# A three-term fp32 encoder: where the second wide tile of the next unit's scores stands

## The reference

```python
def _band_attend(q, k, v, q_pos, k_pos, rel_bias):
    s = jnp.einsum('bqhd,bkhd->bhqk', q, k, ...) * (A_HEAD_DIM ** -0.5)
    ...
    p = jax.nn.softmax(jnp.where(valid, s + bias, NEG), axis=-1)
    return jnp.einsum('bhqk,bkhd->bqhd', p, v.astype(jnp.float32))
...
y = jnp.concatenate([br, mo], axis=-1) * jax.nn.silu(gate)
x = x + y @ w_out[i]
```

## Time and profile before

| | us |
|---|---|
| median of 3 runs | 2897.47 |
| lowest and highest | 2891.87, 2906.21 |
| profiled execution | 2902.79 |
| its span | 2901.0 |
| TensorE busy | 2741.9 (95%) |
| DVE, ACT, POOL busy | 1344.6, 1326.0, 723.6 |
| granted TensorE clock, mean | 0.974 |

### The profile page before, as it was taken

The page is one execution under the profiler, slowest core; times in us unless marked ns, Lnnn a source line. Parts: engine busy times, 40 slices in busy tenths (PEclk is TensorE's granted clock), DMA queues, the critical chain, the costliest instruction groups (busy, mean ns, idle before and its releaser), DMA issues.

```text
span 2901.0 us, 46736 instructions
## 1 busy us (share of the span) xinstructions
PE 2741.9 (95%) x18936; PEld 2570.8 (89%) x18936; DVE 1344.6 (46%) x3237; ACT 1326.0 (46%) x2851; POOL 723.6 (25%) x399
## 2 busy tenths in 40 slices
PE   7999999989999999989999989999899999999897
PEld 5999999879999999979998878888799999999786
DVE  4045555564215565664515255555512055555643
ACT  4244444442325555552334356666523344444521
POOL 0232222234222222221521122222051222222313
PEclk9999999989999999989999999999899999999898
DMA  4111111114211121113311000000232111111111
GB/s 150 55 60 52 47 47 47 50 43 161 68 48 63 56 70 53 59 47 120 103 50 47 26 27 12 13 10 7 86 134 68 48 47 57 47 51 55 52 68 67
DMA packets 58629, 171.98 MB, mean 59 GB/s; under 512 B 6768, under 2 KB 15472, under 8 KB 57904
## 3 DMA queue, kind: packets, MB, share of 16 engines
q1 hardware_dynamic: 58416, 169.01, 16.9%
HBM read 135.06 MB, written 33.92 MB: 58 GB/s over the span
## 4 chain that ended last, share of the span: by engine, by line
PE 76%; ACT 9%; DVE 8%; issue 3%; POOL 3%; DMA 0%; SPq 0%; DVEq 0%; ACTq 0%
PE acc L1876 40%; PE acc L1966 11%; PE turned L1925 6%; PE scores L1909 5%; PE scores L1753 4%; PE acc L1823 4%; ACT prob L1272 3%; DVE prob L1563 2%; PE turned L1753 2%; PE scores L1898 1%; DVE pt_split L1592 1%; PE scores L1730 1%; DVE y_sb L1621 1%; ACT pt_split L1284 1%; POOL w_lo L1652 1%
## 5 line engine op out<-in xcount | busy, mean ns | idle before, releaser
L1876 PE MATMUL acc<-h_split,w_hi 128*128 128x352 f32 (+2 forms) x5220 | 986.5, 330 | 36.3 <-DVE w_rest L1484 9.3
L1876 PEld LDWEIGHTS acc<-h_split,w_hi 128*128 128x128 f32 x5220 | 852.5, 191 | 70.0 <-issue 18.1
L1652 POOL TENSOR_TENSOR w_lo<-w_raw,w_hi 128x1024 fp32r<-128x1024 f32 (+2 forms) x154 | 333.7, 2168 | 1558.6 <-ACT w_hi L1170 1558.6
L1592 DVE TENSOR_TENSOR pt_split<-turned,pt_split 128x512 fp32r<-128x512 f32 (+4 forms) x564 | 303.3, 552 | 537.3 <-ACT pt_split L1284 536.5
L1563 DVE CUSTOM_DVE_ANT_0 prob<-scores,bias 128x256 f32<-128x256 f32 (+9 forms) x576 | 338.0, 633 | 418.6 <-PE scores L1909 395.7
L1876 PE MATMUL acc<-h_split,w_lo 128*128 128x352 f32 (+2 forms) x2610 | 514.6, 325 | 0.0
L1966 PE MATMUL acc<-pt_split,v_split 128*64 128x256 f32 (+5 forms) x3486 | 480.8, 274 | 26.6 <-ACT pt_split L1284 7.9
L1272 ACT ACTIVATE prob<-prob,stat 128x256 f32<-128x256 f32 (+9 forms) x468 | 303.7, 650 | 298.6 <-DVE stat L1563 298.5
L1876 PEld LDWEIGHTS acc<-h_split,w_lo 128*128 128x128 f32 x2610 | 438.1, 190 | 0.0
L1966 PEld LDWEIGHTS acc<-pt_split,v_split 128*64 128x64 f32 (+1 forms) x3486 | 390.1, 155 | 43.9 <-ACT pt_split L1284 14.9
L1284 ACT ACTIVATE pt_split<-turned 128x512 fp32r<-128x512 f32 (+4 forms) x564 | 261.6, 482 | 248.6 <-PE turned L1925 247.5
(11 more groups left out here) (142 smaller groups left out, 2844.3 us busy)
## 6 DMA issues: line engine op xcount, KB each, us to landing
w_raw<-w SPq DMA_DIRECT2D x132, 512.0 KB, 3.7
x_scr<-y_sb SPq DMA_DIRECT2D x24, 528.0 KB, 5.6
y_sb<-x_scr SPq DMA_DIRECT2D x24, 528.0 KB, 7.9
y_sb<-x_in SPq DMA_DIRECT2D x16, 528.0 KB, 10.6
mw_raw<-w SPq DMA_DIRECT2D x16, 512.0 KB, 8.8
bias<-rel_in SPq DMA_DIRECT2D x24, 320.0 KB, 4.2
raw<-kcache SPq DMA_DIRECT2D x18, 256.0 KB, 3.9
v_cache<-vcache SPq DMA_DIRECT2D x18, 256.0 KB, 3.9
```

The costliest lines, as they stand in the source:

```text
L1592: ins = dve.tensor_tensor(pt[0:rows, chunk.p % 2, 1, c0:c0 + n], t_ps[chunk.a % 2][0:rows, c0:c0 + n], pt[0:rows, chunk.p % 2, 0, c0:c0 + ...
L1652: pool.tensor_tensor(w_lo[:, n % 2, 0:wide], w_raw[:, n % 2, 0:wide], w_hi[:, n % 2, 0:wide].bitcast(F32), ALU.subtract).then_inc(wlo_made ...
L1876: ins = pe.matmul(acc[s.bank][:, 0:s.cols], w[ws][:, 128 * k:128 * k + 128], x(xs, k), start=(k, y) == products[0], stop=(k, y) == product ...
```

## The change

One condition loses one term: the second wide tile is now placed behind the second turning in layers A and B too, wherever the present unit has more than one chunk.

```diff
@@ -460,7 +460,7 @@
         if at == 4 and following is not None:
             order.append(("bprep", following))
         narrow = two and max(t.width for t in nxt.tiles) <= 512
-        late_scores = two and not narrow and nxt.job.kind == "C" and n > 1
+        late_scores = two and not narrow and n > 1
         for c in range(n):
             if c == 0 and at == 0 and prev is not None:
                 self.times_v(prev, len(prev.chunks) - 1)
```

## The result

| | before | after |
|---|---|---|
| median of 16 runs, us | 2897.95 | 2905.11 |
| lowest and highest, us | 2891.57, 2906.21 | 2898.77, 2910.93 |
| profiled execution, us | 2902.79 | 2908.76 |
| its span, us | 2901.0 | 2907.0 |
| mean granted clock in it | 0.974 | 0.977 |

The changed kernel is slower: ratio 1.0028, 95% interval 1.0018 to 1.0038, so 5 to 11 us. The forecast was 6 us faster, and the time lies above the range (2883 to 2902). It is inside the bound of 0.5% that I called "within", but clear of the noise and of the other sign.

A forecast was written before the change was run, and what follows sets the result against it. TensorE, busy 95% of the span, was taken as the bound, leaving its idle time and low clock. Waits 2.3 us plus clock 3.7 us gave 6.0 us gained, from the 2897.5 median to 2891.5 us; range 2883 to 2902.

The forecast's parts named there:

- Zero, in all 12: Unit 0 of band jobs: no gain or loss; unit 3's first turning keeps 0.5 us of slack at full clock.
- signs of being wrong: Unit 3's turning waiting in all jobs, new side waits for the bank in jobs with a drop, or differential-layer drops.
- The clock: Band layers: about 4 of 8 clock drops go as shorter jobs slide away, 0.92 us each, 3.7 us gained; bounds 0 to 7.4.
- Third turning of full band jobs: Unit 1: its wait goes, 0.38 us in 7 jobs with a drop; net 0.23 in 3 without, after a query-read wait.
- Last band job: Unit 1, each band layer: third turning's 1.35 us wait becomes a fourth-turning wait 0.3 us dearer, 0.6 us lost in two.
- Differential jobs: Unit 1: first gains 0.3 us, middle four nothing, last loses 0.8 us at the first turning of unit 2.
- "nothing" for the swap: TensorE, all 30 places: exchanging scores and turning costs 0; some 0.2 us either way possible, widening the range by 1 us.
- (a): Rival: the clock drops stay, one in each job, and only the waits count: 2895.2 us; chance 0.2.
- (b): Rival: nearly all eight clock drops go: 2887.8 us; chance 0.15.
- (c): Rival: no effect, the third turning's wait comes back at the fourth everywhere: 2897.5 us; chance 0.09.
- (d): Rival: slower, second tile late on DVE, 0.8 us at 18 unit 1 places, 0.3 at 12 unit 0: 2915.5 us; chance 0.06.
- The rule weighed: Clock drops come from waits of the array for data; by it alone the change would leave all eight.

The follow-up runs named there:

- the three kernels: The changed kernel (0.85 us lost in unit 0), unit0_only (0.86 us a job) and sides_adjacent (0.92 us a job).
- sides_adjacent: Kernel before, with unit 0's second-tile scores in band jobs moved behind the second side and no further: 2906.59 us, ratio 1.0034.
- sides_apart: The change, but in unit 0 of the band jobs the second side stands behind the late scores: 2895.92 us, ratio 1.0000 to before.
- the first four experiments: unit1_only, unit0_only, sides_adjacent and sides_apart, run on the same chip as 21 runs of the kernel before.
- the last two: full_band_jobs and bsum_between, run on the same chip as 21 runs of the kernel before.
- unit1_only: Kernel before, with the second tile's scores late in unit 1 alone (18 places): 2894.64 us against 2896.64, ratio 0.9993.
- unit0_only: Kernel before, with the second tile's scores late in unit 0 of the 12 band jobs alone: 2905.39 us, ratio 1.0035.
- full_band_jobs: Kernel before, with the second tile late in unit 1 of the 10 full band jobs alone: 2896.28 us against 2898.10, ratio 0.999.
- bsum_between: full_band_jobs, plus the sum of squares put between second and third side in differential jobs' unit 0: 2891.66 us against before's 2898.10, ratio 0.9977.

## Why the prediction was wrong

**The step that failed: unit 0 of the band jobs.** I wrote "Zero, in all 12". I followed the moved step to its new place, asked what it would make late there (the first turning of unit 3, 0.5 us of slack) and found nothing; that part held, for no such wait is in after. I never asked what it left behind. It had been the cover of ACT's read between two sides. I even named the 24 products that it moves past, and that all sides share a bank is in the description of the code. The price could be read in advance: the row of 4.9 us in 6 times for `raw`, and its mark of 0.55 us in layer B's unit 0, where three sides stand in a row. 10 x 0.88 (the mean of the 0.85, 0.86 and 0.92 of the three kernels) = 8.8 us. That the two neighbours are the cause is shown by sides_adjacent (the loss with turning and normalising in the old order) and sides_apart (0.64 of 0.85 us gone with all the rest as in after). One of my signs of being wrong was new waits of sides for the bank; I looked for them in unit 1, and they came in unit 0.

**The clock, forecast at 3.7 us gained: no gain shown.** In the profiled executions the drops of the full band jobs fell from seven to two, and the mean granted clock rose from 0.974 to 0.977. The mechanism, that a job of another length slides away from the drops, fits this: the traces of the six experiments, one execution each, have none to four in these ten jobs. The error was to take one execution for the mean, and then to take the gain off the wrong number. I counted drops in an execution that stood 5.3 us above the median, and subtracted their price from the median. The mean granted clock over many executions, by kernel:

| runs | mean granted clock |
|---|---|
| before, beside the first four experiments (21) | 0.9778, from 0.975 to 0.981 |
| before, beside the last two (21) | 0.9766, from 0.973 to 0.980 |
| after (16) | 0.9765 |
| unit1_only (11), unit0_only (5) | 0.9768, 0.9778 |
| sides_adjacent (5), sides_apart (11) | 0.9780, 0.9776 |
| full_band_jobs (11), bsum_between (11) | 0.9773, 0.9756 |

The profiled execution of before, with 0.974, lies below all of the first 21 and near the lowest of the second. A line through the first 21 runs gives 1.5 us for each 0.001 of clock. So 3.7 us gained would be 0.0025 more clock, and after doesn't show it against either group. Nor is a loss shown: the two groups of one kernel differ by 0.0012 themselves, some 2 us. The term should have been 0, with at least those 2 us to both sides.

**What held.** Third turning of full band jobs: timeline of TensorE, unit 1 of job 2, layer 0, of after, and the read of the query side from the timeline of ACT.

```profile
286.08 0.89 PE L1966 MATMUL acc<-pt_split,v_split 128*64 128x256 f32 x6 [0.31 <-DVE v_split L1601]
...
288.74 0.60 PE L1937 MATMUL turned<-ident,raw 128*128 128x128 f32 x4
289.17 0.60 PE L1925 MATMUL turned<-ident,prob 128*128 128x128 f32 x4
289.53 0.95 PE L1966 MATMUL acc<-pt_split,v_split 128*64 128x256 f32 x6
290.56 2.22 PE L1876 MATMUL acc<-h_split,w_hi 128*128 128x352 f32 x12
```

```profile
290.07 0.44 ACT L1131 ACTIVATE q_raw<-acc 128x352 f32<-128x352 f32 x1
```

The turning at 289.17 has no idle mark, where the earlier trace rows have 0.28 and 0.40, and the side at 290.56 starts 1.03 us after the product, where before it is 0.80 (223.41 - 222.61): the forecast wait for the read of the query side, 0.27 by the sum, 0.23 here. What I did not have is the 0.31 us at 286.08: the first product now waits longer for the low half of the values, 0.17 us in the trace of before. Net 0.19 us a job, forecast 0.23. In jobs with a drop 0.45 (67.75 in unit1_only against 68.20), forecast 0.38.

Last band job: the wait moved to the fourth turning, against the earlier trace rows.

```profile
564.74 0.44 PE L1925 MATMUL turned<-ident,prob 128*128 128x128 f32 x2 [1.61 <-DVE v_split L1601]
```

First to fourth turning takes 12.27 us (564.74 - 552.47) and not 12.08 (564.35 - 552.27): 0.2 lost, forecast 0.3.

Differential jobs: the first gains 0.32 us (64.38 against 64.70), forecast 0.3. The middle four lose 0.13 each, forecast 0. There is no new wait in them. The late order itself takes longer: in job 3, from the last eight products ahead of it to the sum of squares behind it, 7.65 us (1041.69 to 1049.34 in unit1_only) against 7.53 (1043.39 to 1050.92). So my "nothing" for the swap did not hold in this layer. The last waits longer at the first turning of unit 2, against the earlier trace rows:

```profile
1248.33 0.66 PE L1925 MATMUL turned<-ident,prob 128*128 128x128 f32 x4 [2.21 <-DVE prob L1585]
```

12.19 us from the job's first turning, 11.41 before: 0.8 lost, as forecast. Over the whole job the comparisons don't agree. unit1_only takes 65.28 us against 65.38 before, with the same mean clock, 0.90. But the drops lie elsewhere. At the turning behind the longest wait of the job it is 0.98 us behind (42.78 us from the job's start against 41.80), with a clock of 0.96 against 0.99 up to there, and it catches up later, with 0.77 against 0.73. And after is 0.78 us behind bsum_between, which has the old order in this unit, at an equal clock of 0.87. The first row is after, the second bsum_between:

```profile
1236.14:1302.98 66.84, 55.05 (x346) 48.32 (x346) 44.06 (x97) 35.89 (x90) 21.00 (x11) 0.87 0.17 51
```

```profile
1226.48:1292.54 66.06, 55.21 (x346) 48.25 (x345) 44.09 (x97) 35.92 (x90) 21.01 (x11) 0.87 0.17 51
```

So how much of the 0.8 us the kernel as a whole bears is open.

With measured terms: 8.8 lost in unit 0, 2 gained in unit 1 (10 x 0.2), 0.3 gained and 0.5 lost in layer B, 0.4 lost in the last band jobs, together 7.4 us lost. The medians say 7.2. With up to 0.8 more from the last differential job it would be 8.2, still inside 5 to 11.

**The rivals.** (a), all drops stay, is not what the profiled execution shows, and (b), nearly all go, did not give its time. (c), the wait that comes back at the fourth turning, holds in the last jobs alone. The slower one, (d), has the right side and a wrong mechanism: unit 3's turning never waits for the normalised tile, and unit 1 gains.

**The rule weighed.** The Trainium skill (TensorE: Matmul & The Clock Gate, section HAM oscillation — how this bites in real kernels) ties drops to waits for data. Here the 3.4 us at 0.50 stand where TensorE is busy throughout, ahead of the first it is busy too (3.40 of 3.40 us in 277.10 to 280.50), and in the trace of after only two of the ten full band jobs have one, though the steps right ahead of that place are the same. By that rule alone all would have stayed, so for these drops the traces decide against it. What brings them is open. The Trainium skill (same page, section What's actually happening) also says that the monitor runs freely; the sliding of the drops agrees, and so does the clock's differing between executions of one program.

## What to carry to other kernels

A step that is moved leaves a hole: look at what its two old neighbours share, here one accumulation bank and the read that empties it, before looking at what it meets in its new place. Where two users of one bank stand next to each other, independent TensorE work put between them takes the place of the wait (here 0.79 us of it where 0.55 us had been idle), and the list of waits shows where such a pair already exists; the best kernel here came from that row. Don't book a gain from fewer clock drops read off one execution: compare the mean granted clock over many.

## What the runs showed of the hardware

One program, two sets of 21 executions: mean granted clock from 0.975 to 0.981 and times from 2891.5 to 2902.1 us in one, 0.973 to 0.980 and 2892.4 to 2908.9 in the other. They go together at 1.5 and 1.8 us for 0.001 (correlation 0.95 and 0.93), so most of the scatter of this kernel goes with the clock. Handing one bank of 352 columns from TensorE over ACT back to TensorE cost 0.63 us of idle time in after: 0.11 from the modelled end of the last product to ACT's start, 0.46 of reading, 0.06 to the next product.
